# Carrying operands across phase boundaries: x kept on chip into select, spread and values as one block, merge's operands made in the last head pair

## The chip, the cores and the metric

The kernel runs on one core of a Trainium2 chip. The metric is the device time of one execution in microseconds (us); the figure for the kernel before is the median of three runs. Engines: PE (TensorE, matmuls; PEld is its weight load), DVE (VectorE), ACT (ScalarE), POOL (GpSimd), and SP (SyncE), which here only issues DMAs.

## What is computed

One decoder layer on a sequence of 1024 tokens of 1024 channels, in float32, and a final norm:

```python
h = rms_norm(x, norm_mix_g[l])
proj = h @ w_in[l]
conv_in, q, k, v, gate_logits = jnp.split(proj, splits, axis=-1)
gates = jax.nn.sigmoid(gate_logits + b_gate[l])
...
conv_out = conformer_conv(conv_in, ...)          # GLU, 31-tap depthwise conv, layer norm, silu, w_conv_out
attn = stick_breaking_attention(q, k, v)         # 16 heads of 64
x = x + (g_conv * conv_out + g_attn * (attn @ w_attn_out[l])) @ w_out[l]
h = rms_norm(x, norm_xattn_g[l])
x = x + memory_cross_attention(h, m, ...)        # 4 heads, 256 memory tokens
h = rms_norm(x, norm_ffn_g[l])
x = x + peer_ffn(h, ...)                         # top 16 of 128*128 experts for each of 8 heads
return rms_norm(x, norm_final_g)
```

In `peer_ffn` each token picks experts by product keys; the sum over them is gate * gelu(u_e . h) * v_e. The kernel computes gelu(U h) for all 16384 experts, multiplies by a dense gate matrix that is zero but for the picked ones, and multiplies by V.

## The kernel before

A value of 1024 channels by 1024 tokens lies as `[P, NC, T]`: 128 partitions, 8 chunks of channels, 1024 tokens. Every large product is made in three passes (lines 155 to 157): operands are split into a high part (fp32r, written by an ACT copy) and a low part (the rest, a subtraction on DVE or, for weights, POOL), and PE adds hi\*hi, hi\*lo and lo\*hi. Products of 512 tokens (`H`) fill one PSUM bank.

The program is a chain of phases. Each is a block with its own semaphores: it starts behind a barrier of all engines (line 75), and ends (lines 79 to 82) when every engine has done its list, which for SP includes waiting for its last stores; then semaphores are cleared behind another barrier. What passes from phase to phase goes through DRAM. Within a phase each engine works its list in order and waits on semaphores.

- **mixer** (from line 193). The loop `pairs` runs over 8 pairs of heads. In the body for pair j the attention of pair j is done in 12 cells (two query halves `qh`, key blocks `kb` from the diagonal down), while PE projects the chunks for pair j+1 between them; the last pair has no projections (`more` is 0). A cell: scores `z` on PE (`z_cell`, for the cell after), ACT makes abs, exp, log (`log_part`), DVE makes softplus (line 588) and log-sigmoid (593), ACT its high part (485), POOL and DVE one low part each (335), PE the running sum `c` (`add_own`, `add_rest`), DVE subtracts (608), ACT takes exp (494), PE weighs the values (`weigh`, 687) into `mix_o`. DVE also runs the 31 taps of the convolution (564), one or two a cell. At the end of each query half ACT copies `mix_o` to `oT` (`outputs`, 506), and SP stores pair j's `oT` (367) at the end of its body.
- **merge** (from 719). Loads the attention outputs chunk by chunk into `part`, makes `ahi` (ACT, 869) and `alo` (DVE, 924), and runs 24 chunks of weights (8 attention, 8 convolution, 8 output). For the first chunk PE waits for each `alo` part. SP issues, in this order: attention chunks, two weight chunks, the first two gates, and the convolution output y as one load of 4 MB (783). DVE reduces y over its chunks (926); PE sums that over partitions behind chunk 1 (844); centring, squares and variance follow on DVE and ACT, and PE adds up the variance behind chunk 4.
- **cross attention** (from 1004). Its last part multiplies by the output weights, 8 chunks of two halves; DVE adds each half to x (1359), and SP stores each chunk as x2 (1087).
- **select** (from 1524). Loads x2 into `front` in four DMAs (1609), then pairs of weight chunks. ACT squares (134), DVE adds (142), PE sums over partitions (147), DVE and ACT make the root (99 to 117) and h; PE starts on the pair products, while POOL prepares sums of the pair's chunks (1412 to 1419). Gelu tiles of 92 of the 128 expert columns go to DRAM.
- **spread** (from 2118). For 8 tiles of 128 tokens DVE makes one-hot matrices and PE spreads the gates by 8 steps each (`step`); ACT stages them, and issues four DMAs of 2 MB for each token tile to `gates` (2258). Between the steps PE makes the remaining 36 expert tiles in halves (`half`): ACT splits `uraw` high (2095), POOL low (2099), ACT takes the gelu (2115) into one of two buffers, SP stores it (2089). The last 8 halves lie behind the last step.
- **expert** (from 2264). 32 groups of 4 expert columns. SP loads gelu tiles `act`, gates `graw` and values `vraw`; DVE multiplies (2409), ACT and DVE split (2379, 2355), ACT and POOL split the values (2373, 2355), PE makes 16 products of 12 matmuls a group, DVE adds them to `acc` (2419). The wait of PE for `added` lets it run four banks ahead. Groups 0 to 30 run in a loop, the last one is written out with the final norm.

The phase that splits its first operands holds PE like this (merge, line 849):

```python
for n in range(NC):
    chunk(n, n % 2, ahi, alo, alo_made if n == 0 else None)
    if n == 1:
        pe.wait_ge(y_summed, 1)
        total(mean, 0, mean_sum)
```

## Time and profile before

| | |
|---|---|
| median of 3 runs | 4884.57 us (4881.81 to 4887.05) |
| the profiled execution, own time | 4880.7 us |
| its span, first to last instruction | 4879.0 us |
| mean granted clock of TensorE | 0.972 |
| PE busy | 4577.1 us (94%) |
| DVE busy | 2829.4 us (58%) |
| ACT busy | 1698.1 us (35%) |
| POOL busy | 1752.8 us (36%) |
| DMA | 555.56 MB, mean 114 GB/s |

The page cuts the span into 40 slices of 122 us; a digit is the busy share in tenths (9 is 90% or more), and PEclk the clock that was granted to TensorE in tenths of full speed.

```profile
PE   6999999978988959999999989999799999999998
DVE  5676767775423346777777737775344444444445
```

Two views need a word. Busy time by stretch: the stretch, its length, then busy time and count of PE, PEld, DVE, ACT and POOL, the granted clock (1.00 is 2.4 GHz, 0.50 is 1.2 GHz), the DMA share and GB/s. Timeline: start, duration, engine, line, operation, output and inputs, shapes, count, and in brackets the idle time before it and what ended that; SPq is SP's queue of DMAs.

### The profile page before, as it was taken

The page shows a single profiled execution, that of the slowest core. Times are in us where ns is not written, and L with a number is a line of the kernel's source. Part 1 is how long each engine was busy: PE and PEld are TensorE (multiplying, and loading weights), DVE is VectorE, ACT ScalarE, POOL GpSimd, SP SyncE. Part 2 cuts the span into 40 slices and gives each one's busy share as a digit, 9 for nine tenths or more (in the row PEclk, how much of TensorE's full clock was granted, in tenths as well). Part 3 has the DMA queues.
Part 4 walks back from the last instruction along what each step waited for, and adds up shares of the span by engine and source line. Part 5 has one row for each costly group of instructions (what it writes and reads, how often), then busy time and mean ns, then how long its engine had stood idle before and what let it go on. Part 6 is the DMA issues. An engine that isn't in the chain of part 4 may idle for free. (4 is left out here: it accounts for less than half of the span.)

```text
span 4879.0 us, 62227 instructions
## 1 busy us (share of the span) xinstructions
PE 4577.1 (94%) x21768; PEld 3659.9 (75%) x21768; DVE 2829.4 (58%) x4467; ACT 1698.1 (35%) x2690; POOL 1752.8 (36%) x1078
## 2 busy tenths in 40 slices
PE   6999999978988959999999989999799999999998
PEld 4766666646767748888888878888688888888886
DVE  5676767775423346777777737775344444444445
ACT  3555555563423323333333334333211111111111
POOL 1443444421223017777777751111222222222221
PEclk9999999988999979999999999999899999999999
DMA  2111111114432122222222325555644444444441
GB/s 79 44 48 48 46 47 48 39 39 151 155 129 78 56 104 83 99 95 95 97 96 103 110 100 185 216 215 212 224 145 146 150 139 145 145 145 148 141 145 63
DMA packets 260000, 555.56 MB, mean 114 GB/s; under 512 B 17104, under 2 KB 148432, under 8 KB 246736
## 3 DMA queue, kind: packets, MB, share of 16 engines
q1 hardware_dynamic: 255184, 485.85, 29.8%
q10 hardware_dynamic: 4608, 67.11, 3.3%
q8 instruction: 109, 1.79, 0.2%
q14 instruction: 99, 0.81, 0.1%
HBM read 384.08 MB, written 168.82 MB: 113 GB/s over the span
## 5 line engine op out<-in xcount | busy, mean ns | idle before, releaser
L155 PE MATMUL expert_o<-expert_ahi,expert_vhi 128*128 128x512 f32 x2048 | 799.1, 390 | 25.2 <-POOL expert_vlo L2355 20.2
L157 PE MATMUL expert_o<-expert_ahi,expert_vlo 128*128 128x512 f32 x2048 | 798.1, 390 | 0.0
L156 PE MATMUL expert_o<-expert_alo,expert_vhi 128*128 128x512 f32 x2048 | 798.1, 390 | 0.0
L2419 DVE TENSOR_TENSOR expert_acc<-expert_acc,expert_o 128x512 f32<-128x512 f32 x496 | 340.8, 687 | 712.1 <-PE expert_o L157 707.0
L2355 POOL TENSOR_TENSOR expert_vlo<-expert_vraw,expert_vhi 128x1024 fp32r<-128x1024 f32 x128 | 323.9, 2531 | 1053.9 <-ACT expert_vhi L2373 1053.9
L155 PEld LDWEIGHTS expert_o<-expert_ahi,expert_vhi 128*128 128x128 f32 x2048 | 385.3, 188 | 107.5 <-issue 26.6
L157 PEld LDWEIGHTS expert_o<-expert_ahi,expert_vlo 128*128 128x128 f32 x2048 | 385.2, 188 | 80.2
L156 PEld LDWEIGHTS expert_o<-expert_alo,expert_vhi 128*128 128x128 f32 x2048 | 385.3, 188 | 80.1 <-issue 0.2
L2379 ACT ACTIVATE expert_ahi<-expert_act 128x1024 fp32r<-128x1024 f32 x128 | 135.8, 1061 | 727.9 <-DVE expert_act L2409 727.9
L155 PE MATMUL mix_gemm<-mix_hhi,mix_w_hi 128*128 128x512 f32 x896 | 361.9, 404 | 23.9 <-POOL mix_w_lo L185 13.5
L157 PE MATMUL mix_gemm<-mix_hhi,mix_w_lo 128*128 128x512 f32 x896 | 358.4, 400 | 0.0
L156 PE MATMUL mix_gemm<-mix_hlo,mix_w_hi 128*128 128x512 f32 x896 | 358.3, 400 | 0.0
L155 PE MATMUL select_products<-h_hi,select_hi 128*128 128x512 f32 x864 | 339.1, 393 | 16.1 <-DVE h_lo L1845 12.8
L156 PE MATMUL select_products<-h_lo,select_hi 128*128 128x512 f32 x864 | 338.0, 391 | 0.0
L564 DVE SCALAR_TENSOR_TENSOR mix_room<-mix_u,mix_cwj,mix_room 128x1024 f32<-128x1024 f32 x240 | 323.5, 1348 | 6.3 <-DVE mix_u L536 3.2
L1432 POOL TENSOR_TENSOR select_raw_low<-select_raw,select_hi 128x1024 fp32r<-128x1024 f32 x108 | 278.3, 2577 | 15.5 <-ACT select_hi L1443 11.4
L2373 ACT ACTIVATE expert_vhi<-expert_vraw 128x1024 fp32r<-128x1024 f32 x128 | 134.8, 1054 | 386.5 <-PE expert_o L157 382.5
L155 PE MATMUL select_products<-select_t_hi,select_hi 128*128 128x512 f32 x648 | 253.9, 392 | 15.8 <-DVE select_t_lo L1859 11.9
L1432 POOL TENSOR_TENSOR select_s_low<-select_s,select_hi 128x512 fp32r<-128x512 f32 x108 | 219.1, 2029 | 114.3 <-ACT select_hi L1443 114.3
L157 PE MATMUL select_products<-h_hi,select_raw_low 128*128 128x512 f32 x648 | 254.0, 392 | 0.0
L156 PE MATMUL select_products<-select_t_lo,select_hi 128*128 128x512 f32 x648 | 252.9, 390 | 0.0
L2099 POOL TENSOR_TENSOR spread_ulo<-spread_uraw,spread_uhi 128x1024 fp32r<-128x1024 f32 x36 | 94.1, 2616 | 425.8 <-ACT spread_uhi L2095 425.8
(319 smaller groups left out, 9916.4 us busy)
## 6 DMA issues: line engine op xcount, KB each, us to landing
gates<-spread_stage ACTq DMA_DIRECT2D x32, 2048.0 KB, 15.1
expert_act<-gelu_u SPq DMA_DIRECT2D x128, 512.0 KB, 3.4
expert_graw<-gates SPq DMA_DIRECT2D x128, 512.0 KB, 4.6
expert_vraw<-in_peer_v SPq DMA_DIRECT2D x128, 512.0 KB, 6.4
select_raw<-in_select_pairs SPq DMA_DIRECT2D x54, 1024.0 KB, 5.0
gelu_u<-front SPq DMA_DIRECT2D x184, 256.0 KB, 2.0
mix_w_raw<-in_w_mix SPq DMA_DIRECT2D x56, 512.0 KB, 3.7
spread_uraw<-in_peer_u SPq DMA_DIRECT2D x36, 512.0 KB, 4.6
```

The costliest lines, as they stand in the source:

```text
L155: nc.tensor.matmul(out, whi, xhi, start=(first and i == 0), stop=False)
L156: nc.tensor.matmul(out, whi, xlo, start=False, stop=False)
L157: mm = nc.tensor.matmul(out, wlo, xhi, start=False, stop=(last and i == len(terms) - 1))
L564: nc.vector.scalar_tensor_tensor(out=ybuf[:, par], in0=u[:, par, t:t + T], scalar=cwj[:, par, t:t + 1], in1=ybuf[:, par], op0=ALU.mult, op ...
L1432: self.nc.gpsimd.tensor_tensor(low, src, high.bitcast(F32), ALU.subtract).then_inc(self.lo_made, 1)
L2099: self.nc.gpsimd.tensor_tensor(self.lo[:, n % 3], self.raw[:, n % 3], self.hi[:, n % 2].bitcast(F32), ALU.subtract).then_inc(self.lo_made, 1)
L2355: return eng.tensor_tensor(low, raw, high.bitcast(F32), ALU.subtract)
L2373: nc.scalar.activation(vhi[:, q], vraw[:, q], ACT.Copy).then_inc(vhi_made, 1)
L2379: nc.scalar.activation(ahi[:, par, e], act[:, e], ACT.Copy).then_inc(ahi_made, 1)
L2419: nc.vector.tensor_tensor(acc[:, k, h * H:h * H + H], acc[:, k, h * H:h * H + H], ops[:, d, h], ALU.add).then_inc(added, 1)
```

## The change

**x kept on chip into select.** `front`, the buffer that select works in, is allocated before cross attention, and that phase keeps x and its norm's scratch there. Its last Fori loops over output chunks are written out. After each half of an output chunk is added, ACT squares it (`square_out`) and DVE adds the square to `x_total` (`sum_square`). Chunks 0 to 6 of x2 are stored as before, chunk 7 is stored by select. Select loads no x; PE sums `x_total` over partitions as soon as the constants are made, and DVE's gain step on chunk 7 waits for the store.

**Spread and values in one block.** `expert_phase` becomes part of `spread_value_phase`; its buffers lie over those of spread that are free by then (`act`, `vraw`, `vlo` over `front`; `graw`, `vhi`, one `ahi`, `alo` over `stage`; `acc` and the other pair over `h_hi`, `h_lo`). Group 0 is written out instead of group 30. SP, ACT and PE do parts of it beside the last 8 expert halves (`beside`), the first two chunks of x go to `x_first`, and the gelu output has three buffers instead of two.

**Merge's operands in the last head pair.** The mixer's `hhi`, `hlo` and weight buffers are shared with merge as `ahi`, `alo` and its weight buffers. In the last pair, which projects nothing, SP reloads attention chunks 0 to 6 (`next_stage`), ACT makes high parts in cells 1 to 7, DVE low parts in cells 2 to 8; the first two weight chunks of merge are loaded, ACT and POOL split them in cells 8 and 9. The last pair's own output goes straight from PSUM to `ahi` and `alo`, not to DRAM. Merge loads gates, then y, and waits for no operand. The tensors that both phases share lie in an outer phase, which adds a barrier at its end.

```diff
 # mixer, SP
+            def next_stage():
+                sync.wait_ge(group_done, NG * NC)
+                for b in range(2):
+                    sync.wait_ge(evicted[b], NB * NC + 1)
+                for k in range(NC - 1):
+                    sync.wait_ge(o_stored[k % 2], 16 * (k // 2 + 1) + 1)
+                    if k >= 2:
+                        sync.wait_ge(alo_made, k - 1)
+                    sync.dma_start(part[:, k % 2], attn_out[:, k]).then_inc(a_loaded[k % 2], 16)
+                    if k == 2:
+                        sync.wait_ge(w.lo_made, NW * NC)
+                        for n in range(2):
+                            sync.dma_start(w.raw[:, n], w_next[n]).then_inc(next_loaded, 16)
 # mixer, ACT, in cell i behind sp_hi and before log_part
+                    if not more and i in ATTN_HIGH_AT:          # i = 1 to 7
+                        k = ATTN_HIGH_AT[i]
+                        act.wait_ge(a_loaded[k % 2], 16 * (k // 2 + 1))
+                        nc.scalar.activation(ahi[:, k], part[:, k % 2], ACT.Copy).then_inc(ahi_made, 1)
+                    if not more and i in NEXT_AT:               # 8, 9: w.hi; POOL: w.lo behind low_part
...
 # mixer, DVE, in cell i behind low_part and before the taps
+                    if not more and i in ATTN_LOW_AT:           # i = 2 to 8
+                        k = ATTN_LOW_AT[i]
+                        dve.wait_ge(ahi_made, k + 1)
+                        nc.vector.tensor_tensor(alo[:, k], part[:, k % 2], ahi[:, k].bitcast(F32), ALU.subtract).then_inc(alo_made, 1)
+                    if not more and i == 5:
+                        own_low(0)
...
+                if not more:
+                    own_low(1)
 # mixer, PE
-                if opens[i]:
+                if opens[i] and not more and qh:
+                    pe.wait_ge(own_low_made, 2)
+                elif opens[i]:
                     pe.wait_ge(o_copied, 4 * j + 2 * qh + 1)
 # merge, SP
-            sync.dma_start(part[:, 0], attn_in[:, 0]).then_inc(a_loaded[0], 16)
-            w.load(sync, wstream, 0, 0, first=True)
...
+            for s in range(2):
+                sync.dma_start(gate[:, s], gate_in[:, s]).then_inc(g_loaded[s], 16)
             sync.dma_start(xy[:], y_in).then_inc(y_loaded, 16)
 # cross attention, ACT and DVE, behind each output half
+                nc.scalar.activation(sq[:, h, 0:H] if k else x_total[:, hs], xq[:, k, hs], ACT.Square).then_inc(x_squared, 1)
...
+                nc.vector.tensor_tensor(x_total[:, hs], x_total[:, hs], sq[:, i % 2, 0:H], ALU.add).then_inc(x_summed, 1)
 # select, SP
-            for i in range(4):
-                sync.dma_start(xT[:, 2 * i:2 * i + 2, :], x_in[:, 2 * i:2 * i + 2, :]).then_inc(x_loaded[i], 16)
-            for n in range(2):
-                pr.load(sync, n)
+            pr.load(sync, 0)
+            sync.dma_start(x_out[:, NC - 1], xT[:, NC - 1]).then_inc(x_stored, 16)
+            pr.load(sync, 1)
 # spread and values, SP; half counts the last 8 halves from 0
+            def beside(half):
+                if half == -1:
+                    sync.wait_ge(gated, 2 * N)
+                    sync.wait_ge(one1_made, N)
+                    sync.wait_ge(g_done, N * NB)
+                    for k in range(QC):
+                        sync.dma_start(x_first[k][:], x_in[:, k]).then_inc(x_loaded[0], 16)
+                    load_tile(0, ds(0, 1), None)
+                    load_values(0, ds(0, 1), None)
+                if half == 3:
+                    load_tile(1, ds(1, 1), None)
+                if half == 4:
+                    sync.wait_ge(stored, 16 * NS * NT)
+                    load_gates(0, ds(0, 1))
+                    load_gates(1, ds(1, 1))
+                    for e in range(2, E):
+                        load_tile(e, ds(e, 1), None)
+                        load_gates(e, ds(e, 1))
+                    for q in range(1, NQ):
+                        load_values(q, ds(0, 1), None)
...
+            sync.wait_ge(ex.done, 2 * TILES)
+            for q in range(1, NQ):
+                part = slice(q * QC, q * QC + QC)
+                sync.dma_start(acc[:, part], x_in[:, part]).then_inc(x_loaded[q], 16)
 # spread and values, ACT
+            def beside(half):
+                if half == 5:
+                    act_eng.wait_ge(stored, 16 * NS * NT)
+                    values(0, 0)
+                    for e in range(2):
+                        weighted_high(0, 0, e)
+                if half == 6:
+                    for e in range(2, E):
+                        weighted_high(0, 0, e)
+                    values(0, 1)
+                if half == 7:
+                    values(0, 2)
+                    values(0, 3)
```

## Rows read from the trace of the kernel before

**Rows 1.** PE's waits: line, waited for: us in total, times, longest us

```profile
PE merge_banks L155 <- DVE merge_alo L924: 27.2, 7, 17.2
...
PE select_products L147 <- DVE front L142: 21.8, 1, 21.8
...
PE expert_o L155 <- POOL expert_vlo L2355: 20.2, 1, 20.2
...
PE merge_sums L844 <- DVE merge_part L954: 6.0, 1, 6.0
```

**Rows 2.** Busy time by stretch, each engine (count), granted clock, DMA share, GB/s

```profile
1006.00:1058.00 52.00, 38.65 (x139) 22.84 (x140) 44.60 (x69) 34.30 (x84) 22.16 (x38) 0.68 0.03 11
...
1058.00:1081.00 23.00, 18.13 (x62) 7.20 (x60) 18.39 (x27) 17.02 (x33) 5.10 (x4) 0.98 0.06 22
...
3455.00:3475.00 20.00, 14.68 (x45) 10.91 (x46) 9.56 (x7) 5.04 (x6) 7.87 (x4) 0.65 1.06 388
...
3600.00:3700.00 100.00, 100.00 (x443) 82.81 (x442) 47.26 (x57) 19.61 (x19) 22.64 (x9) 1.00 0.45 142
```

**Rows 3.** Timeline, cross attention to select: start us, us, engine, operation, [idle]

```profile
1763.65 0.69 DVE L1359 TENSOR_TENSOR xattn_xq<-xattn_xq,xattn_gemm 128x512 f32 x1 [4.73 <-PE xattn_gemm L157]
...
1768.87 1.94 SPq L1609 DMA_DIRECT2D front<-x  x4
...
1785.26 3.75 PE L147 MATMUL select_products<-front,select_ones 128*128 128x512 f32 x4 [21.75 <-DVE front L142]
...
1789.04 1.29 DVE L99 TENSOR_SCALAR front<-select_products 128x512 f32<-128x512 f32 x2 [3.93 <-PE select_products L147]
...
1793.65 2.36 POOL L1432 TENSOR_TENSOR select_raw_low<-select_raw,select_hi 128x1024 fp32r<-128x1024 f32 x1 [3.52 <-ACT select_hi L1443]
...
1793.85 3.24 DVE L115 TENSOR_TENSOR front<-front 128x1024 f32<-128x1024 f32 x1
```

**Rows 4.** Timeline, mixer to merge

```profile
1083.46 0.59 ACT L506 ACTIVATE mix_oT<-mix_o 64x512 f32<-64x512 f32 x1 [0.36 <-PE mix_o L687]
...
1088.39 0.34 SPq L773 DMA_DIRECT2D merge_part<-attn  x1
...
1120.15 1.23 DVE L924 TENSOR_TENSOR merge_alo<-merge_part,merge_ahi 128x1024 fp32r<-128x1024 f32 x1 [1.34 <-ACT merge_ahi L869]
...
1128.93 14.84 DVE L926 TENSOR_REDUCE merge_mean<-merge_xy 128x1024 f32<-128x8192 f32 x1 [7.55 <-DMA merge_xy<-conv]
...
1143.82 3.21 PE L844 MATMUL merge_sums<-merge_mean,merge_ones 128*128 128x512 f32 x4 [2.32 <-DVE merge_mean L926]
```

**Rows 5.** Timeline, cells 4 and 5 of the last head pair

```profile
1034.63 0.71 DVE L608 TENSOR_TENSOR mix_logw<-mix_logsig,mix_c 128x128 f32<-128x128 f32 x2 [0.93 <-PE mix_c L665]
...
1037.43 0.76 PE L687 MATMUL mix_o<-mix_weight,mix_room 128*64 128x128 f32 x4 [1.34 <-ACT mix_oT L506]
...
1038.58 0.65 DVE L335 TENSOR_TENSOR mix_sp_lo<-mix_softplus,mix_sp_hi 128x256 fp32r<-128x256 f32 x1 [0.72 <-ACT mix_sp_hi L485]
...
1039.48 0.87 ACT L468 ACTIVATE mix_expz<-mix_z 128x384 f32<-128x384 f32 x2 [0.94 <-PE mix_z L157]
```

**Rows 6.** DMA issues: count, KB each, median us to landing

```profile
merge_xy<-conv SPq DMA_DIRECT2D x1, 4096.0 KB, 13.3
...
xattn_xq<-x SPq DMA_DIRECT2D x1, 4096.0 KB, 12.2
...
expert_graw<-gates SPq DMA_DIRECT2D x128, 512.0 KB, 4.6
```

**Rows 7.** Timeline, spread to values

```profile
3418.39 0.60 ACT L2115 ACTIVATE spread_ugelu<-spread_a 128x512 f32<-128x512 f32 x1 [10.11 <-DMA gelu_u<-spread_ugelu]
...
3435.35 0.39 PE L157 MATMUL spread_a<-h_hi,spread_ulo 128*128 128x512 f32 x1
...
3464.84 0.77 PE L155 MATMUL expert_o<-expert_ahi,expert_vhi 128*128 128x512 f32 x1 [4.03 <-DVE expert_alo L2355]
```

**Rows 8.** Loads of `spread_uraw` from 3380 to 3440 us

```profile
DMA to landing us min/median/max: 4.8/8.9/13.1
```

548 lines of the change are left out of this document (293 added, 255 removed).

## The prediction

> **What bounds the kernel now.** I read the page first: TensorE (PE) is busy for 94% of the 4879.0 us span, DVE for 58%, so a change is worth what it takes out of PE's gaps, and 4577 us of PE work stay. The list of PE's waits then says where gaps of over 10 us are. Three of the longest are seams, the places where one phase ends and the next begins: 27.2 us on `merge_alo` (in 7 pieces), 21.8 us before the sum of squares of select, 20.2 us before the first value matmul; a fourth entry, 6.0 us in merge, shows that DVE and not PE leads there for a while [rows 1]. The view of busy time by stretch gives the rate of undisturbed work: 443 matmuls in 100 us at a granted clock of 1.00, or 0.226 us each, and behind a seam 45 matmuls in 20 us at 0.65 [rows 2]. The timelines around the three seams give the terms. I price each seam as the time by which the same piece of work comes earlier.
>
> **Seam 1, cross attention to select.** Before, the last output add starts at 1763.65 and takes 0.69 us; its store lands, the barrier passes, and select issues its first DMA at 1768.87. Select loads x, squares and adds it, and PE sums it at 1785.26; DVE goes on with the mean at 1789.04 [rows 3]. Now x lies in `front`, and the total of squares is made beside the output products. Sixteen squares of 512 columns (0.6 us each on ACT, as [rows 7]) and fifteen adds (0.69) fall into gaps of 4.7 us between DVE's output adds, so I cost them at nothing but the tail: behind the last add come one queued add, and one square plus one add in series, 1.5 us. The end of the phase no longer holds a store. From the old last add (1764.34) to the first issue of select were 4.5 us, of which the last 1.9 are barriers behind the store's landing. New start: 1764.34 + 1.5 + 1.9 = 1767.7. The constants that PE waits for are there 0.8 us behind that (POOL makes `ident` 0.4 us into the phase and takes 0.3), and PE's sum took 3.8 us to DVE's reading: DVE goes on at 1772.3, **16.7 us** earlier. The load of the first pair now lands about 11 us earlier, so four POOL sums (1.3 us each) come to lie over DVE's three steps that finish the root. Before, one of those steps took 3.24 us beside a POOL operation of 2.36 [rows 3], where such an operation takes 1.23 undisturbed [rows 4]: 2 us lost. Now up to three steps can each lose up to 1.3, so I add 1 us (0 to 3). Store of chunk 7, gains and keys (2.6 MB in all, ahead of `c_loaded`) are needed 14 us into the phase and cost nothing. Seam 1: **-15.7 us** (-13 to -17).
>
> The row of 3.24 us agrees with what the Trainium skill says in SBUF — State Buffer, SBUF: two separate sides: the port pair of DVE and GpSimd is an exclusive lock, taken also by a DVE operation with two SBUF inputs, and the loser blocks for the whole instruction. It speaks against this edit; by it alone the three steps would lose 3.9 us at most instead of 2.0, and the seam would be worth 1 us less than my sum.
>
> **Seam 2, mixer to merge.** Two things change. (a) The last head pair gets more work: 7 high parts on ACT (1.06 us) and 7 low parts on DVE (1.23 [rows 4]), the pair's own high and low parts (0.59 and about 0.69, four each), and two weight chunks (1.05 on ACT, 2.4 on POOL). DVE is busy 44.60 of 52 us in the first eight cells of this pair and 18.39 of 23 in those behind [rows 2]. So in cells 2, 3, 6 and 7 a low part adds its full 1.23, 4.9 us together. In cell 4 DVE waits 0.93 us for `mix_c` [rows 5], so only 0.3 is added; in cell 8, where DVE has some 1.6 us of slack, nothing to 0.3. ACT's additions fit its gaps (it waits 1.0 us in each of these cells). Cell 5 is the dear one, since the change adds a wait. PE's `weigh` of cell 4 used to wait for ACT's copy (start 1037.43 [rows 5]); now it waits for `own_low(0)`, which stands on DVE behind the low part of cell 5 and one attention low part. From the old start 1038.58 of that low part: 0.65 + 1.23 + 2 x 0.69 gives 1041.9, so `weigh` moves by 4.5 us. Behind it in PE's queue stand the scores of cell 6, for which ACT waits (1039.48 [rows 5]), and the sum for cell 5, for which DVE waits. Cell 5 grows by **4.5 us**, in which its DVE additions are contained. The DMAs (seven of 0.5 MB and two of weights, landing in 3.9 us) have a cell of 6 to 7 us each. Sum (a): 4.9 + 0.3 + 4.5 + 0.3 = **+10 us** (4 to 25: from half of the low parts hidden, to every added ACT, DVE and POOL operation in series, 7 x 1.06 + 7 x 1.23 + 4 x 0.69 + 2 x 1.05 + 2 x 2.4).
>
> (b) The end of the phase: ACT's last copy starts at 1083.46 and ends at 1084.05, the store follows, and merge issues at 1088.39 [rows 4]. Now `own_low(1)` (1.45) replaces the store: 1084.05 + 10 + 1.45 + 1.9 = 1097.4. PE starts merge 0.6 us behind that at once, instead of piecemeal until 1121. But what is late next is the mean: PE may go on with chunk 2 only when DVE has reduced y, and that ended before at 1143.8 (start 1128.93, 14.84 us), where PE had waited 2.3 [rows 4]. y's load now goes out second, behind two gate loads of 0.5 MB. A load of 4 MB took 12.2 us alone and 13.3 behind 0.5 MB [rows 6]; behind 1 MB, and issued 0.9 us into the phase, it lands at 0.9 + 12.2 + 2.2 = 15.3 us. Reduced: 1097.4 + 15.3 + 14.9 = 1127.6, against 1143.8, **16.2 us** earlier, and the chain behind it (centre, squares, variance) leads until PE's wait of 6.0 us, so it shifts whole. PE itself has run 24 us by then and stands for 6; it comes back at the low clock, and a chunk that ends later holds DVE's products: 1.6 us lost (0 to 3). Seam 2: **-14.6 us** (0 to -20).
>
> The Trainium skill (DMA: Bandwidth & Descriptors, Anatomy of one DMA — SWDGE (gpsimd) path) fits a DMA by 2.0 us and 436 GB/s. By that page the 5.24 MB would be there in an estimated 14.0 us instead of 15.3, and the seam would be worth 1.3 us more. No row here shows the path that the page measured, so the sum stays with the rows.
>
> **Seam 3, spread to values.** Before, the last spread matmul starts at 3435.35 and the chain of four operand tiles lets the value matmuls run steadily from 3464.84; by 3475.0 45 are done [rows 2, 7]. With all inputs ready these 45 (10.2 us) would be done at 3445.2 if PE lost nothing (the third `ugelu` buffer also removes the 0.7 us that PE lost when ACT waited 10.11 us for a store [rows 7]). So at most 29.8 us are to be had. What holds them back: the gate tiles can be loaded only when the 8.4 MB of the last token tile are stored. The change puts 2.1 MB ahead of them, 5 us at the 388 GB/s of a full queue [rows 2]. The weights of the last tile, issued at 3402.2, took 13.1 us to land [rows 8]; now they land at 3420.3 and POOL has them split at 3423.9, just when PE wants them: no stall, and nothing in reserve. The store for which ACT waited until 3418.39 [rows 7] shifts alike to 3423.4, so SP passes its waits and issues the gate loads at about 3424.6; the first lands 4 us later (4.6 [rows 6]) at 3428.6. Then DVE, ACT, DVE make four tiles in turn, 3.7 us each (1.23 + 1.06 + 1.23 and hand-overs): the fourth is ready at 3443.4, while PE, free at 3435.0, wants it at 3437. PE loses 6.7 us in pieces and about 2 us by the low clock it comes back with (45 matmuls in 20 us at 0.65 before). The loads of the second group stand on SP behind the last `ugelu` store and 3 MB of `acc`, arrive near 3456, and DVE's second add queues behind them; four banks cover it within 1 us. Seam 3: 29.8 - 8.7 = **-21 us** (-12 to -27).
>
> **Small terms.** One more barrier, at the end of the shared tensors, is +0.4. The value loop has the same waits, counts and buffers, and PE is busy for 100.00 of 100 us in it [rows 2]: 0.
>
> **Sum.** 15.7 + 14.6 + 21 - 0.4 = 51 us. The profiled execution took 4880.7 us: 4829.6. The median shown is 3.9 us above that execution, so I forecast **4833.5 us** as a median.
>
> **Rivals.** *The last head pair is strained* (a at its upper bound): for it speaks DVE's load; against it the gaps of ACT and POOL. 15 us less gained: 4849; chance 0.14. *The value operands come late*: the gate stores, and with them the loads, slip further, or the last weights stall PE; for it speaks that the same bytes had stores waiting over 10 us, against it that the shift is 5 us and no more bytes follow. 12 us less: 4845; chance 0.12. *More is hidden*: the pair grows by 5 us only and the four value tiles cost PE 3: 11 us more: 4822; chance 0.08. *Nothing moves*: the waits that replace the old ones eat all three gains, 4885; chance 0.02. *Slower*: the value loop, 31 more groups of 43 us, loses by its new order of loads in SP's queue. It decides from 51 / 31 = 1.6 us a group; at 2.5 us it gives 4833 + 77 = 4911. Against it: DMA is busy for 0.45 there and PE never waits [rows 2]. Chance 0.02. My forecast has 0.62.
>
> **Range.** It takes in the forecast with its bounds and the first three rivals: 4819 to 4856. A measurement tells about 0.2% (10 us) from no change. Faster 0.96, same 0.02, slower 0.02.
>
> **What would show it.** In the changed profile: PE's sum in select less than 2 us after that phase's first DMA, and no square behind it; `weigh` of cell 4 in the last pair waiting for DVE, and this pair some 10 us longer; the reduction in merge starting about 15 us into the phase with PE waiting 5 to 7 us for it; three gaps of 1 to 4 us between the first value matmuls. Wrong would be: a pair longer by 20, a wait for `spread_ulo` at the last tile, or waits inside the value loop.

## The result, and where the profile after differs

The changed kernel took 4817.82 us (median of 4 runs, 4815.81 to 4819.57) against 4885.5 for the kernel before (4 runs); the ratio is 0.9863, 95% interval 0.9851 to 0.9875. That is 67.7 us less where 51 were forecast, and 1.2 us below the low end of the range. The profiled execution took 4819.57 us, its span fell from 4879.0 to

```profile
core 0: 4817.9 us, clock 0.977
```

The first thing to make of two such traces is a table of the same piece of work in both. These rows of the timeline of after are the marks: the start of cell 1 in the last head pair, the first issue of merge, its reduction, the first issues of cross attention and of select, the mean of select, the first product, the last matmul of spread, the first of values.

```profile
997.30 0.75 DVE L646 SCALAR_TENSOR_TENSOR mix_softplus<-mix_z,mix_ln 128x256 f32<-128x256 f32 x2
...
1083.49 0.80 SPq L840 DMA_DIRECT2D merge_gate<-logits  x2
...
1099.71 14.55 DVE L976 TENSOR_REDUCE merge_mean<-merge_xy 128x1024 f32<-128x8192 f32 x1 [18.26 <-DMA merge_xy<-conv]
...
1396.41 0.33 SPq L1120 DMA_DIRECT2D xattn_mem<-in_mem  x1
...
1741.18 0.34 SPq L1478 DMA_DIRECT2D select_raw<-in_select_pairs  x1
...
1745.73 1.29 DVE L99 TENSOR_SCALAR front<-select_products 128x512 f32<-128x512 f32 x2 [6.38 <-PE select_products L1737]
...
1760.51 0.76 PE L155 MATMUL select_products<-h_hi,select_hi 128*128 128x512 f32 x1 [14.82 <-DVE h_lo L1913]
...
3391.66 0.39 PE L157 MATMUL spread_a<-h_hi,spread_ulo 128*128 128x512 f32 x1
3391.89 0.39 PE L155 MATMUL spread_g<-spread_ahi,spread_vhi 128*128 128x512 f32 x1
```

Before, the marks of select and of the last spread matmul stand in [rows 3, 7], merge's first issue and its reduction in [rows 4]; the others of before are

```profile
1009.87 0.75 DVE L588 SCALAR_TENSOR_TENSOR mix_softplus<-mix_z,mix_ln 128x256 f32<-128x256 f32 x2
...
1424.21 0.33 SPq L1068 DMA_DIRECT2D xattn_mem<-in_mem  x1
...
1801.62 0.76 PE L155 MATMUL select_products<-h_hi,select_hi 128*128 128x512 f32 x1 [12.61 <-DVE h_lo L1845]
```

| mark | before | after | lead, us | gained since the mark above |
|---|---|---|---|---|
| last head pair, cell 1 | 1009.87 | 997.30 | 12.6 | **12.6** |
| first issue of merge | 1088.39 | 1083.49 | 4.9 | -7.7 |
| y reduced (start and duration) | 1143.77 | 1114.26 | 29.5 | +24.6 |
| first issue of cross attention | 1424.21 | 1396.41 | 27.8 | -1.7 |
| first issue of select | 1768.87 | 1741.18 | 27.7 | -0.1 |
| mean of select | 1789.04 | 1745.73 | 43.3 | +15.6 |
| first product of select | 1801.62 | 1760.51 | 41.1 | -2.2 |
| first matmul of spread (the trace has its row) | 2909.69 | 2868.64 | 41.1 | 0.0 |
| last matmul of spread | 3435.35 | 3391.66 | 43.7 | +2.6 |
| last matmul of values (3455.97 and 3391.89 were the first) | 4859.0 | 4797.7 | 61.3 | +17.6 |

The first line decides the case: 12.6 us lie in a part of the mixer that the change does not touch. Seven head pairs ran before that mark, with the same instructions. The busy time of PE says the same: 4577.1 us before, 4558.8 after, 18.3 less with the same 21768 matmuls. The three seams together gave 48.7 us, where 51.3 were forecast.

The table compares one profile with one profile, so its small differences are not to be trusted: seven kernels of this study run the same instructions up to merge's first issue with the same matmul durations (after, a_two, a_yfirst, a_loads, a_poolwait, a_pad128, a_both32), and it stands between 1081.87 and 1084.84 in them.

PE's waits over the whole kernel after:

```profile
PE merge_sums L902 <- DVE merge_mean L976: 6.3, 1, 6.3
PE merge_sums L902 <- DVE merge_part L1004: 6.0, 1, 6.0
...
PE mix_o L755 <- DVE shared_wide_lo L635: 5.9, 1, 5.9
...
PE select_products L1737 <- POOL select_ident L1715: 4.7, 1, 4.7
...
PE spread_g L155 <- DVE spread_alo L2367: 4.3, 2, 2.5
...
PE spread_g L155 <- DVE spread_acc L2431: 3.0, 1, 3.0
```

The 27.2, 21.8 and 20.2 us of [rows 1] are gone. In their place stand what was forecast: 6.3 us for the mean and 6.0 again in merge, 5.9 for `own_low`, 4.7 for the constants of select, 4.3 in pieces for the operand tiles. The last row, 3.0 us, was not.

### The profile page after: what moved, and what is told of

Read it like the earlier page. It is cut to its first block and busy times, and to the rows that moved or that the text cites. A ratio compares the mean times of both kernels' runs of the same rounds, so it can differ in the third digit from the quotient of the medians.

```text
span 4817.9 us, 62187 instructions
## 1 busy us (share of the span) xinstructions
PE 4558.8 (95%) x21768; PEld 3658.8 (76%) x21768; DVE 2825.8 (59%) x4477; ACT 1698.1 (35%) x2697; POOL 1756.5 (36%) x1078
## 5 line engine op out<-in xcount | busy, mean ns | idle before, releaser
L155 PE MATMUL spread_g<-spread_ahi,spread_vhi 128*128 128x512 f32 x2048 | 799.1, 390 | 7.9 <-DVE spread_alo L2367 4.3
L156 PE MATMUL spread_g<-spread_alo,spread_vhi 128*128 128x512 f32 x2048 | 798.4, 390 | 0.0
L157 PE MATMUL spread_g<-spread_ahi,spread_vlo 128*128 128x512 f32 x2048 | 798.4, 390 | 0.0
L2431 DVE TENSOR_TENSOR spread_acc<-spread_acc,spread_g 128x512 f32<-128x512 f32 x492 | 338.3, 688 | 705.0 <-PE spread_g L157 705.0
L155 PEld LDWEIGHTS spread_g<-spread_ahi,spread_vhi 128*128 128x128 f32 x2048 | 385.5, 188 | 89.6 <-issue 5.4
L157 PEld LDWEIGHTS spread_g<-spread_ahi,spread_vlo 128*128 128x128 f32 x2048 | 385.4, 188 | 80.0
L156 PEld LDWEIGHTS spread_g<-spread_alo,spread_vhi 128*128 128x128 f32 x2048 | 385.4, 188 | 80.1 <-issue 0.2
L155 PE MATMUL mix_gemm<-shared_wide_hi,shared_w_hi 128*128 128x512 f32 x896 | 357.9, 399 | 23.7 <-POOL shared_w_lo L188 14.0
L155 PE MATMUL select_products<-h_hi,select_hi 128*128 128x512 f32 x864 | 339.2, 393 | 18.3 <-DVE h_lo L1913 15.0
L156 PE MATMUL mix_gemm<-shared_wide_lo,shared_w_hi 128*128 128x512 f32 x896 | 354.1, 395 | 0.0
L157 PE MATMUL mix_gemm<-shared_wide_hi,shared_w_lo 128*128 128x512 f32 x896 | 354.0, 395 | 0.0
```

Of the source, the lines that this page charges most:

```text
L155: nc.tensor.matmul(out, whi, xhi, start=(first and i == 0), stop=False)
L156: nc.tensor.matmul(out, whi, xlo, start=False, stop=False)
L157: mm = nc.tensor.matmul(out, wlo, xhi, start=False, stop=(last and i == len(terms) - 1))
L2431: nc.vector.tensor_tensor(acc[:, k, h * H:h * H + H], before[:, h * H:h * H + H], ops[:, d, h], ALU.add).then_inc(added, 1)
```

## Experiments on the mixer's 12.6 us

The rows of a tile group its instructions by line: minimum, median and maximum of the duration in ns, then first and last start. For the projection matmuls of the mixer (2688 of 128x512 in three lines; one line stands here) before and after read

```profile
L156 PE MATMUL mix_gemm<-mix_hlo,mix_w_hi x896: 389/396/632, 37.2 to 999.9; 128*128 128x512 f32 x180
```
```profile
L156 PE MATMUL mix_gemm<-shared_wide_lo,shared_w_hi x896: 386/389/629, 36.9 to 987.3; 128*128 128x512 f32 x180
```

The median is 396 ns before and 389 after; the starts of neighbours stand 0.233 us apart before and 0.227 after. 2688 times 6.5 ns is 17.5 us, near the 18.3 by which PE's busy time fell; 12.6 of them reach the mark. That the rest is lost again in cells that other engines lead is my reading, which no run shows. Nothing in these instructions differs. What differs is the address of the weights: the change allocates `w_hi` at 90240 bytes in each partition, right behind `hlo`; before it was at 167584, behind a gain tile of 32 bytes. `hhi` is at 16512 in both. Pads in either kernel ask which property of the address counts.

```
b_pad, b_224, b_480 (before):   +  m.sb("pad", [P, 8])      # 8, 56 or 120 floats
                                   w = WeightStream(nc, m)
b_wfirst (before): the same w = WeightStream(nc, m) moved up, behind hhi and hlo
a_shift, a_w64 (after):         +  m.sb("pad", [P, 8])      # 8 or 16 floats
                                   weights = WeightStream.buffers(m)
                                +  m.sb("pad2", [P, 8])     # 8 or 16
a_both32 (after):               +  m.sb("pad", [P, 8])
                                   wide = m.sb("wide_hi", ...), m.sb("wide_lo", ...)
                                   weights = WeightStream.buffers(m)
                                +  m.sb("pad2", [P, 24])
a_x32b (after): pad of 8 ahead of wide, pad2 of 24 between wide and weights
b_x32b (before): pad of 8 ahead of hhi, hlo, and pad2 of 24 behind them
```

**b_pad, b_wfirst, a_shift.** Is it the address at all, and is it the odd 32 bytes?

> The kernel before, with an unused tile of 32 bytes per partition ahead of the mixer's weight buffers: w_raw, w_hi and w_lo (and the tiles behind them) move by 32 bytes, from 159392 to 159424, and nothing else changes. Theory address: in before the median projection matmul of the mixer took 396 ns, in after 389, and what changed for it is where its weights lie, 32 bytes off a multiple of 64 in before and on one in after. Then this kernel alone shows 389 ns and is 12 us faster than before (4873). Rival region: it is the place of the buffers in the memory as a whole (159392 against 82048), not the 32 bytes: 396 ns stay and the time is before's within 3 us.

> The kernel before, with the mixer's weight buffers allocated right behind hlo, at 82048, where after has them; everything that stood between them moves up by 24 KB; no instruction is added or removed. Both theories on the place of the weights (the 32 bytes, or the region) expect 389 ns for the median projection matmul and 12 us less than before (4873), the last head pair starting near 997.6 instead of 1009.9. Rival: the gain in the mixer came from something else in after (its last pair, its queues); then this is before's time within 3 us.

> The kernel after, with 32 unused bytes ahead of the shared weight buffers and 32 behind them: the weights of mixer and merge lie at 82080 instead of 82048, all other tiles keep their remainder by 64. Theory address: the projections of the mixer and all of merge's matmuls go to 396 ns, +12 us in the mixer and up to 1152 matmuls x 6.5 ns = 7 us in merge: 4830 to 4837. Rival region: nothing changes, 4818.

b_wfirst took 4871.05 us (8 runs; ratio to before 0.9975, 0.9965 to 0.9986): 389 ns, and merge begins at 1075.79 instead of 1088.39. So the gain belongs to the place of the weights and can be had without the change (4871.05 against 4884.61 for before, 17 runs). a_shift took 4836.24 (4 runs), 18 more than after, with the mixer's matmuls at 395 ns and merge's at 396; its profile lies 12.3 us behind after's at merge's first issue and 2.1 more behind merge. b_pad refuted the simple form: a multiple of 64, and still 394 ns and no gain (4885.15).

**a_w64, a_both32.** By 128, then, and is it the weights' own remainder or that of both operands?

> The kernel after, with 64 unused bytes ahead of the shared weight buffers and 64 behind them: the weights lie at 82112, a multiple of 64 but not of 128; all other tiles keep their remainder by 128. So far: weights at remainder 32 by 128 took 396 and 395 ns (before, a_shift), at remainder 64 took 394 (b_pad), at 0 took 389 (after, b_wfirst), each with the projections' other operand at remainder 0. Theory remainder by 128: 394 ns in mixer and merge, about 10 us slower than after. Rival, that 64 suffices and b_pad was slow for where its other tiles came to lie: 389 ns, 4818.

> The kernel after, with 32 unused bytes ahead of the shared operand tiles and 96 behind the weights: ahi and alo (hhi and hlo) and the weights all lie at remainder 32 by 128, everything behind them as in after. In before's value stage both operands lay at remainder 32 and its matmuls took 389 ns. Theory relative: what counts is that the two operands have the same remainder, so 389 ns, 4818. Theory absolute: the weights' own remainder counts and the value stage was spared by something else (its weights' rows of 256 columns), so 395 to 396 ns in mixer and merge, 4832 to 4836.

a_w64: 394 ns, 4838.19. a_both32: 389 ns, 4819.76 (one run each). In a_both32 the weights' own remainder is 32 as in a_shift, so it is not the weights alone.

The trace of a_both32 has a control inside one run. Merge multiplies the same weight buffers in 16 of its 24 chunks by `wide`, which moved with them, and in 8 by `zhi` and `zlo`, which moved by 128 bytes where the weights moved by 32:

```profile
L156 PE MATMUL merge_banks<-shared_wide_lo,shared_w_hi x256: 387/389/632, 1085.2 to 1391.8; 128*128 128x512 f32 x128
```
```profile
L155 PE MATMUL merge_banks<-merge_zhi,shared_w_hi x128: 392/399/796, 1198.4 to 1297.3; 128*128 128x512 f32 x128
```

The other two passes of the second kind have medians of 392 and 394 ns; in after, where all of them lie at remainder 0, the three stand at 389.

**b_x32b, a_x32b.** Equal remainders by 128, made from the other side.

> The kernel before, with 32 unused bytes ahead of hhi and hlo and 96 behind them: in the mixer the other operand of the projections, not the weights, moves, to remainder 32 by 128; the weights stay at remainder 32 as in before, everything else keeps its remainder, no instruction changes. Theory difference (the two operands' remainders must be equal): 389 ns instead of 396, and the 12 us that after gained in its mixer, 4873. Theory weights' own remainder: 396 ns stay, 4885.

> The kernel after, with 32 unused bytes ahead of the shared operand tiles and 96 between them and the weights: ahi and alo (hhi and hlo) at remainder 32 by 128, the weights at 0. Theory difference: 395 or 396 ns in mixer and merge, 4834 to 4838 as a_shift. Theory weights' own remainder: 389 ns, 4818.

a_x32b gave 397 ns and 4833.05 (one run), as the theory of a difference had it (its products with `zhi`, which moved by 128 bytes like the weights, take 390). b_x32b did not go by that theory: both remainders are 32 and the median is 393, the time 4882.31 (10 runs; ratio 0.9991, 0.9981 to 1.0001). That theory fell in this form. The operands of b_x32b are 151168 bytes apart, a distance whose remainder by 256 is 128; in every kernel with 389 ns this remainder is 0, also in the stages of before that had looked like exceptions (merge 139264, values 65536).

**b_480, b_224.** The new form was written down before these ran.

> The kernel before, with 480 unused bytes ahead of the mixer's weights: the distance in bytes from hhi to w_hi becomes 151552, a multiple of 512. Over all kernels so far the median of the 128x512 projection matmul goes with the remainder of this distance by 512: 0 in after, b_wfirst, a_both32, before's merge and its value stage, 389 ns; 32 in before and a_shift, 396 and 395; 64 in b_pad and a_w64, 394; 96 in a_x32b, 397; 128 in b_x32b, 393. Theory distance: 389 ns and, as in b_wfirst, 12 us less than before (4873), with the weights still high in the memory. Rival region: only the place near 82048 makes it 389; then 393 to 397 and before's time.

> The kernel before, with 224 unused bytes ahead of the mixer's weights: the distance from hhi to w_hi becomes 151296, whose remainder by 256 is 0 and by 512 is 256. If the distance counts by 256, this is 389 ns and 4873 as b_480; if by 512, it is 393 to 397 ns and before's time.

Both came out as it says: 389 ns (rows of b_480 and b_x32b below), 4872.25 us for b_480 (9 runs; ratio 0.9977, 0.9967 to 0.9986) and 4867.6 in one run for b_224, with the weights high in the memory as before. So the distance counts by 256, not by 512, and the region does not. In their profiles merge begins at 1078.64 and 1075.43.

```profile
L156 PE MATMUL mix_gemm<-mix_hlo,mix_w_hi x896: 387/389/632, 36.9 to 989.1; 128*128 128x512 f32 x180
```
```profile
L156 PE MATMUL mix_gemm<-mix_hlo,mix_w_hi x896: 387/393/628, 36.9 to 999.4; 128*128 128x512 f32 x180
```

| distance from `hhi` to `w_hi`, by 256 | kernels | median ns | PE busy, us |
|---|---|---|---|
| 0 | after, b_wfirst, a_both32, b_480, b_224 | 389 | 4558.8, 4561.8, 4559.9, 4565.4, 4561.8 |
| 32 | before, a_shift | 396, 395 | 4577.1, 4578.0 |
| 64 | b_pad, a_w64 | 394 | 4578.1, 4577.4 |
| 96 | a_x32b | 397 | 4577.8 |
| 128 | b_x32b | 393 | 4578.5 |

The last column is PE's busy time over the whole kernel. The kernels made from before (where the mixer alone is moved) have 4561.8 to 4565.4 at remainder 0 and 4577.1 to 4578.5 at 32, 64 and 128; those made from after (mixer and merge) 4558.8 and 4559.9 at 0, and 4577.4 to 4578.0 at 32, 64 and 96. In neither is a lower median among the slow ones worth anything: 393 or 394 ns cost PE as much as 396, and b_pad gained nothing. Remainders of 160 to 224 were not tried for `hhi` and the weights.

**a_pad128** asked the same of `mix_o`, plain float32 with 64 columns of weights, where `v` and `weight` are 32 apart (before the form by 256 was known, so it made them 128 apart).

```
   g_sb = m.sb("gain", [P, NC])
+  m.sb("pad", [P, 24])
```

> The kernel after, with the mixer's 32-byte gain tile followed by 96 unused bytes, so that every operand of the mixer's matmuls lies at remainder 0 by 128 and no pair of operands differs. In after only mix_o is such a pair: v at remainder 0, weight at 32; its 128x512 matmuls run as plain float32, 592 ns median. Theory: the remainder's cost applies there too and is about 6 to 14 ns per matmul of 384, and mix_o is off the limit in most cells, so at most 3 us; mix_c (both at 32, then both at 0) stays. Rival: the cost is one of the projections' kind alone: mix_o stays at 592 ns and the time at 4818.

592 ns stayed, 4820.37 us (4 runs). With a distance of 0 (a_best2, below) it was 592 ns as well. This figure is the median of all 384 `mix_o` matmuls, half of which are 128x512 and the others narrower; minimum and maximum (272, and 1115 to 1116) stayed too. So this kind does not show the effect.

## Experiments on the seams

**a_weigh: the wait for own_low.** In the pair, rows of after around cell 5 (timeline):

```profile
1025.60 0.75 DVE L646 SCALAR_TENSOR_TENSOR mix_softplus<-mix_z,mix_ln 128x256 f32<-128x256 f32 x2
...
1029.41 1.40 DVE L635 TENSOR_TENSOR shared_wide_lo<-mix_o,shared_wide_hi 64x512 fp32r<-64x512 f32 x2
...
1033.65 0.85 DVE L672 TENSOR_TENSOR mix_logw<-mix_logsig,mix_c 128x256 f32<-128x256 f32 x2 [1.52 <-PE mix_c L731]
...
1035.62 1.01 DVE L646 SCALAR_TENSOR_TENSOR mix_softplus<-mix_z,mix_ln 128x384 f32<-128x384 f32 x2
```
```profile
1030.87 0.76 PE L755 MATMUL mix_o<-mix_weight,mix_room 128*64 128x128 f32 x4 [5.86 <-DVE shared_wide_lo L635]
```

```
   (in body of TensorE, ahead of the project calls of cell i)
+  if not more and i == 5:
+      for s in range(2): weigh(j, par, s, 4, more)
   ...
-  for s in range(2): weigh(j, par, s, i, more)
+  if more or i != 4:
+      for s in range(2): weigh(j, par, s, i, more)
```

> The kernel after, where TensorE in the last head pair issues weigh of cell 4 behind z_cell and add_own of cell 5 instead of ahead of them, so that nothing stands behind its wait of 5.86 us for own_low. The prediction laid 4.5 us of the last pair on this wait. If it is the wait, cell 5 (10.02 us in after, 5.74 in before) falls by about 4 and the kernel is 4 us faster. Rival: VectorE's own work is the limit of cell 5 (from its start at 1025.60 to the end of its own operations at 1034.2 with 1.5 us of it waiting for mix_c): then only 1.5 us come back.

```profile
1025.45 0.75 DVE L646 SCALAR_TENSOR_TENSOR mix_softplus<-mix_z,mix_ln 128x256 f32<-128x256 f32 x2
...
1032.03 0.75 DVE L672 TENSOR_TENSOR mix_logw<-mix_logsig,mix_c 128x256 f32<-128x256 f32 x2
...
1033.89 1.02 DVE L646 SCALAR_TENSOR_TENSOR mix_softplus<-mix_z,mix_ln 128x384 f32<-128x384 f32 x2
```
```profile
1030.73 0.77 PE L755 MATMUL mix_o<-mix_weight,mix_room 128*64 128x128 f32 x4 [1.33 <-DVE shared_wide_lo L635]
```

Cell 5 lasted from 1025.45 to 1033.89, 8.4 us instead of 10.0, and `logw` no longer waits. So of the 4.3 us by which the cell had grown 1.6 were the wait; the other 2.7 are as much as DVE's own added work (1.21 for the attention low part and 1.40 for `own_low`), which the prediction had thought contained in the wait. The end of the pair moved by 0.2 only (merge at 1083.30 instead of 1083.49): PE's last `mix_o` group began 1.1 us earlier, but took 3.00 us instead of 2.07, at a granted clock of 0.66 from 1075 to 1080 where after has 1.00. The kernel took 4819.7 (4 runs, 4815.1 to 4820.71), no measurable difference.

**a_yfirst: the two gate loads ahead of y.**

```
+  sync.dma_start(xy[:], y_in).then_inc(y_loaded, 16)
   for s in range(2):
       sync.dma_start(gate[:, s], gate_in[:, s]).then_inc(g_loaded[s], 16)
-  sync.dma_start(xy[:], y_in).then_inc(y_loaded, 16)
```

> The kernel after, where merge loads y ahead of the two gate tiles. In after y is issued 0.85 us into the phase behind 1 MB of gates and VectorE's reduction of it starts 16.2 us into the phase; TensorE waits 6.3 us for the mean. Theory: y's start and the queue's 1 MB both count: the reduction starts 2.5 to 3.5 us earlier in the phase and so does everything to the next such wait: 2.5 us faster. Rival: all 5 MB share the queues and land together, so the order changes under 1 us.

```profile
PE merge_sums L902 <- DVE merge_mean L976: 2.6, 1, 2.6
```

The reduction begins 12.4 us into the phase (1097.19 behind 1084.77) instead of 16.2, and PE's wait fell from 6.3 to 2.6 us, so the mean does lead there, as forecast. From merge's first issue to cross attention's pass 306.6 us; in after 312.9. The one run took 4814.71.

**a_poolwait: GpSimd beside VectorE in select.** The mean came 15.6 us earlier, the first product 13.4. The rows between, DVE and then POOL, of after:

```profile
1749.27 1.62 DVE L112 SCALAR_TENSOR_TENSOR front<-front 128x1024 f32<-128x1024 f32 x1 [2.26 <-ACT front L108]
1750.92 2.17 DVE L115 TENSOR_TENSOR front<-front 128x1024 f32<-128x1024 f32 x1
1753.12 2.17 DVE L117 SCALAR_TENSOR_TENSOR front<-front 128x1024 f32<-128x1024 f32 x1
1755.32 4.44 DVE L1921 SCALAR_TENSOR_TENSOR front<-front,select_gain 128x1024 f32<-128x1024 f32 x2
```
```profile
1748.53 1.27 POOL L1489 TENSOR_TENSOR select_s<-select_raw 128x512 f32<-128x512 f32 x1
...
1751.97 2.24 POOL L1492 TENSOR_TENSOR select_s<-select_raw,select_s 128x512 f32<-128x512 f32 x1
```

```
+  pool.wait_ge(h_made, 1)
   prepare(0, 0, 0)
```

> The kernel after, where GpSimd waits for the first h of select before it makes the sums of the first pair. In after, GpSimd's sums ran from 1747.2 to 1757.5 beside VectorE's norm, and the six VectorE operations from 1749.27 took 1.62, 2.17, 2.17, 2.22 us where before they took 1.23; from the mean's start to the first product 14.78 us passed against 12.58 before. Theory contention: with GpSimd silent these operations take 1.2 to 1.3 us again and the first h_hi comes about 2.2 us earlier, though PE's first product may wait for GpSimd's split instead, so that the time need not fall. Rival: the durations come from something else (the tiles' new places): they stay at 1.6 to 2.2.

```profile
1745.28 1.23 DVE L112 SCALAR_TENSOR_TENSOR front<-front 128x1024 f32<-128x1024 f32 x1 [2.25 <-ACT front L108]
1746.54 1.22 DVE L115 TENSOR_TENSOR front<-front 128x1024 f32<-128x1024 f32 x1
1747.80 1.23 DVE L117 SCALAR_TENSOR_TENSOR front<-front 128x1024 f32<-128x1024 f32 x1
1749.06 2.48 DVE L1922 SCALAR_TENSOR_TENSOR front<-front,select_gain 128x1024 f32<-128x1024 f32 x2
```

With POOL silent the same five DVE operations (the last row holds two) take 6.16 us instead of 10.40, and the first `h_hi` comes 8.6 us behind the mean instead of 12.9. It is contention, and it costs 4.2 us in after. Before, one operation lost 2.0 of it [rows 3]. The step's cost is the difference, 2.2, where I had added 1. PE gains nothing from silencing POOL, since its first product then waits 20.05 us for POOL's split (`select_raw_low`), and the one run took 4818.88.

**a_two: the third buffer of the activated tiles.**

```
-  s = (2 * n + h) % 3            (store)      +  s = (2 * n + h) % 2
-  s, before = ... % 3, ... // 3  (activate)   +  s, before = ... % 2, ... // 2
...
```

> The kernel after with two result buffers for the activated tiles of spread instead of three (the third stays allocated, unused). The stretch from the first to the last matmul of spread was 2.6 us shorter in after than in before, where the prediction gave the third buffer 0.7. Theory: all of it is the third buffer (ACT no longer stands before a store, so the copies into stage come sooner; PE's waits for stage fell from 9.5 to 6.5 us): this kernel is 2 to 3 us slower than after, with waits for stage near 9.5 us. Rival: it is the new placement of the tiles or run-to-run variation: within 1 us of after, waits near 6.5.

4828.89 us (4 runs, 4827.36 to 4830.32), 11 more than after. Spread, from first to last matmul, takes 534.1 us here and 523.0 in after (525.7 before). PE's waits in that stretch, after first:

```profile
PE spread_a L155 <- POOL spread_ulo L2170: 14.4, 2, 13.2
PE spread_g L2508 <- ACT spread_stage L2601: 6.5, 16, 0.4
```
```profile
PE spread_g L2508 <- ACT spread_stage L2601: 9.1, 21, 0.8
PE spread_a L155 <- ACT spread_ugelu L2187: 5.5, 2, 4.1
```

Neither theory had its size. The waits for `stage` are back at 9.1 (9.5 before), which is the 2.6 us that spread gained. But a further 5.5 us of waits for `ugelu`, with a granted clock of 0.53 for 5 us behind the longest (4.1 us), show a second use of the buffer (`ulo` gives 1.2 back, 13.2 for 14.4). ACT stood 9.22 us for a store before that tile, as it had stood 10.11 before the change [rows 7], and now PE has to wait for it. I had counted the buffer as 0.7 and the 2.1 MB that the change puts ahead of the last stores as free. With two buffers on both sides spread takes 8.4 us longer than before (534.1 against 525.7). I lay these 8.4 on that load, which the third buffer then hides; no run takes the load away alone, so its share is argued, not shown. What the buffer is worth in after, 11 us, is shown.

**a_loads: what the second value group waits for.** The start of values in after: PE, then the first gate loads on SP and what DVE waited for, then the busy times of the stretch behind (columns as in [rows 2]):

```profile
3395.23 0.47 PE L155 MATMUL spread_g<-spread_ahi,spread_vhi 128*128 128x512 f32 x1 [1.82 <-DVE spread_alo L2367]
...
3398.71 0.76 PE L155 MATMUL spread_g<-spread_ahi,spread_vhi 128*128 128x512 f32 x1 [2.48 <-DVE spread_alo L2367]
...
3415.44 0.50 PE L155 MATMUL spread_g<-spread_ahi,spread_vhi 128*128 128x512 f32 x1 [3.00 <-DVE spread_acc L2431]
```
```profile
3380.17 1.18 SPq L2307 DMA_DIRECT2D spread_graw<-gates  x2
...
3413.56 1.23 DVE L2420 TENSOR_TENSOR spread_act<-spread_act,spread_graw 128x1024 f32<-128x1024 f32 x1 [12.44 <-DMA spread_graw<-gates]
```
```profile
3415.00:3420.00 5.00, 4.56 (x13) 3.62 (x14) 4.54 (x6) 1.97 (x2) 2.03 (x1) 0.66 1.09 344
```

```
   (load_acc(q) is the loop body that loaded part q of acc; the loop itself goes)
+  for e in range(E):
+      load_tile(e, ds(E + e, 1), e + 1); load_gates(e, ds(E + e, 1))
+      if e in (0, 2): load_acc(e // 2 + 1)
+  for q in range(NQ):
+      load_values(q, ds(1, 1), q + 1)
+      if q == 0: load_acc(3)
   for s in range(3):
       sync.wait_ge(ex.stored[s], 16 * (2 * TILES // 3))
-  with sync.Fori(0, NG - 1) as g:
+  with sync.Fori(1, NG - 1) as g:
```

> The kernel after, where SP issues the second value group's tiles, gates and values between the three loads of acc, ahead of its wait for the last stores of the activated tiles, instead of behind all of it. In after VectorE stood 12.44 us before the first gate product of the second group (until 3413.56), and TensorE 3.0 us at 3415.44 for the sum behind it. The prediction held this to be covered within 1 us. Theory: without that queue ahead of them the gates land near 3405, TensorE's wait of 3.0 us and the low clock behind it are gone, 3 to 4 us. Rival: acc, now later, takes the place of the gates: the same wait under another name, within 1 us of after.

PE's wait for `acc` is gone, DVE stands 4.89 us for the gates instead of 12.44, and from the first to the last hi\*hi value matmul pass 1403.3 us instead of 1405.4. The 3.0 us are not all gained: the waits for the value tiles (`spread_alo`) add up to 5.5 us instead of 4.3. The one run took 4813.67.

**a_best, a_best2: together.** Both have a_weigh, a_yfirst and a_loads; behind `gain` stands a pad of 96 bytes in a_best and of 480 in a_best2.

> The kernel after with four edits together: the operands' remainders made equal, weigh of cell 4 behind add_own of cell 5, y ahead of the gates in merge, and the second group's loads ahead of the wait for the last stores. Sum of what each should bring by the runs and traces so far: 0 to 3, 0.2 (the end of the pair moved by 0.2 in a_weigh), 2.5, 3: 6 to 9 us faster than after, 4809 to 4812. Rival: pieces hide each other, the clock falls where waits go, under 4 us.

> a_best with the pad behind gain 480 bytes instead of 96. In after, a_pad128 and a_best the distance from the value tile v to weight had the remainder 32, 128 and 128 by 512, and mix_o's 128x512 matmuls took 592 ns in all of them; here it is 0. If the distance counts for plain float32 with 64 columns of weights too, mix_o falls below 592 ns and up to 3 us are gained on a_best (4811.6); if not, 592 ns and the same time within 2 us.

a_best took 4811.59 us (4 runs; ratio to before 0.985, 0.9833 to 0.9866), a_best2 4807.77 (5 runs, 4803.34 to 4811.88; ratio 0.9842, 0.9829 to 0.9855). The latter is 10 us below after, and its runs (to 4811.88) do not reach after's (from 4815.81), though the intervals of the two ratios overlap. The median of `mix_o` is 592 ns in both, so the pad is not what tells them apart. The stretch from the first issue of cross attention to that of select, which no experiment edits, took 342.9 to 347.1 us in the profiles of this study (344.7 before, 344.8 in after), so that much of a difference between two single profiles of the same phase is not the edit's.

## Why the prediction was wrong in size and right in kind

Against the profiled execution the sum gave 4829.6; it took 4819.57, 10.0 us less. The median adds 5.7 to this: I laid 3.9 on the profiled execution, as it had been before, but after's median is 1.75 below its profiled run.

| term | forecast | measured | |
|---|---|---|---|
| mixer ahead of the last pair | 0 | -12.6 | the missing term |
| seam 2, mixer to merge | -14.6 | -15.2 | 27.8 - 12.6 |
| seam 1, cross to select | -15.7 | -13.3 | 41.1 - 27.8 |
| seam 3, spread and its end | -21 | -20.2 | 61.3 - 41.1 |
| barrier and the end | +0.4 | +0.2 | 61.3 to 61.1 in the span |

**The step that failed** stands in the prediction's first paragraph: that a change is worth what it takes out of PE's gaps, "and 4577 us of PE work stay". They did not: PE was busy for 4558.8 us. The new address of a buffer had no term in the sum, not even one of 0. The prediction priced what waits for what, and left the duration of the matmuls as [rows 2] had it. In its place the runs show 12.6 us in the mixer ahead of all seams. b_wfirst (13.6 us by the medians), b_480 (12.3) and b_224 (17.0 in one run) take them out of the kernel before by moving buffers alone, and a_shift (18 more) and a_w64 (20 more in one run) put them back into after. This settles the cause as the distance of the operands' addresses; why the matmuls are slower then is open. Without these 12.6 us the profiled execution would have taken some 2.6 us more than the sum, not 10 less.

**Seam 2** was near in its sum, in part by luck. The pair grew by 8.5 us (cell 1 to the end of ACT's last copy: 74.2 before, 82.7 after) against 10; cell 5 by 4.3 against 4.5. The reason given for cell 5 was in the main wrong: in a_weigh only 1.6 of it went with the wait. Cells 2, 3, 6 and 7 grew by 3.3 us together, not 4.9 (from the starts of softplus; cell 2, for one, took 6.92 before and 8.00 after). Cell 8 grew by 1.6 instead of 0.3; by these rows its low part ran into POOL's split of the next weights:

```profile
1055.14 3.39 DVE L658 TENSOR_TENSOR shared_wide_lo<-mix_room,shared_wide_hi 128x1024 fp32r<-128x1024 f32 x1
```
```profile
1054.93 2.52 POOL L445 TENSOR_TENSOR shared_w_lo<-shared_w_raw,shared_w_hi 128x1024 fp32r<-128x1024 f32 x1 [0.27 <-ACT shared_w_hi L530]
```

POOL ends at 1057.45; 1.21 us, what the DVE operation takes alone, from there gives 1058.66, and it ended at 1058.53. That agrees with what the Trainium skill says (SBUF — State Buffer, SBUF: two separate sides): the loser waits out the whole instruction. The reduction began 16.2 us into the phase against 15.3, behind a pair that ended earlier; y was reduced 16.9 us earlier by the seam's own, against 16.2.

**Seam 1**: the mean 4.55 us behind the first issue, as forecast (4.6); no squares behind it. Mis-sized was POOL's overlap, +2.2 for +1 (a_poolwait): I counted three steps, but the two that apply the norm lay under it too. The other 1.2 us are missing at select's first issue, which was to come 1.2 us earlier and came 0.1 later by the seam's own; this is less than the stretch ahead of it varies between profiles. In select both engines slow down, POOL too (1.27 alone, 2.24 beside DVE). The prediction's estimate of at most 3.9 us for the three steps, by the lock that the Trainium skill describes (SBUF — State Buffer, SBUF: two separate sides), would have been too much: against a_poolwait they lost 2.3 (5.96 us for 3.68), and the two gain steps behind them the other 2.0.

**Seam 3** had errors that nearly cancel, which is luck. Spread became 2.6 us shorter, not 0.7, and by a_two the third buffer did far more than that: without it spread is 11.1 us longer than in after and 8.4 longer than before. At the start of values the two gaps of 1.8 and 2.5 us are less than the 6.7 forecast, for the gate loads went out 11.5 us ahead of PE's last spread matmul, not 10. But "four banks cover it within 1 us" was wrong: DVE stood 12.44 us for gates of the second group, and PE lost 3.0 us and then came back at a granted clock of 0.66 for 5 us (a_loads). The wait for `spread_ulo` at the last tile, named as a sign against me, is there with 1.2 us (14.4 less the 13.2 at the start). In the value loop PE waits for nothing, before (3480 to 4850 us) as after (3430 to 4790).

Two slips of the prediction changed nothing here: the upper bound for the pair adds up to 25.7, and the bounds of the three seams together give 4821 to 4860, not 4819 to 4856. Of the rivals, none had the right cause. "More is hidden" came nearest in size (4822), with a pair that grew by 8.5, not by 5; its reason is not the one that acted.

## What to carry to other kernels

Where a change moves buffers, compare the durations of the untouched matmuls and PE's busy time first: 6 or 7 ns in 390 are invisible in a list of waits and were worth as much here as a seam. Lay the weights and the moving operand of a long float32r product at a distance that is a multiple of 256 bytes; a gain tile of 32 bytes between them undid it. And ask of a moved load what it does to the stores queued behind it: here the kernel needed a third store buffer beside it, and is 11 us slower without.

## What the runs showed of the hardware that was not expected

The 128x512 float32r matmul with 128x128 weights takes 389 ns when the addresses of its two operands within the partition differ by a multiple of 256 bytes, and 393 to 397 at the remainders 32, 64, 96 and 128 (table above; 392 to 399 over the three passes with `zhi` in a_both32), in the mixer and in merge; the granted clock from 500 to 600 us is 1.00 before and after alike. PE's busy time over the kernel does not tell these remainders apart. Plain float32 with 64 columns of weights kept its median of 592 ns at remainders 0, 32 and 128. VectorE and GpSimd working side by side in SBUF slow each other: 10.40 us for 6.16 on one, 2.24 for 1.27 on the other.
